# Selected attention: GpSimd weighs two of the four selected heads, and ScalarE's selected exponentials are split around the first window copies

## The chip, the core and the metric

One core of a Trainium2 chip runs the whole program: TensorE (PE, with its weight loads as PEld), VectorE (DVE), ScalarE (ACT), GpSimd (POOL) and SyncE (SP), each with its own instruction queue, tied together by semaphores. The metric is the device time of one execution in microseconds (us); smaller is better.

## The reference

The input (512 tokens of width 1024, float32) goes through two blocks of differential attention with a conformer convolution, and then through a block that mixes a gated delta rule with native sparse attention (NSA), projects, and ends in a squared-ReLU MLP. The change touches only the NSA part: 16 query heads in 4 groups of 4, head width 64.

```python
o_cmp = einsum(softmax(s_c) * any_valid, vc)          # compressed keys
o_slc = selection_branch(q, k_s, v_s, sel_idx, slopes) # selected blocks of 64 keys
o_win = window_branch(q, k_w, v_w, slopes)             # the last 256 keys
gates = sigmoid(gate_logits).reshape(B, S, G, R, 3)
o = gates[..., 0:1] * o_cmp + gates[..., 1:2] * o_slc + gates[..., 2:3] * o_win
```

With 512 keys there are 8 blocks and 8 are selected, so the selected branch is full causal attention. Each branch's softmax is divided by its sum and multiplied by its gate; the kernel does both with one factor per query and head ("weighing") before the probabilities go to PE.

## The kernel before

The NSA attention runs over 16 units, `units[u] = (g, t)`: a head group g of 0 to 3 and, inside it, a tile t of 128 queries, 0 to 3. A unit has 128(t+1) selected keys, at most 384 window keys and 31 compressed ones, for 4 heads (`REP`). Each engine's program is written out by hand, and the engines work one unit apart: while PE, and ACT's copies, finish unit u, DVE and ACT prepare unit u+1.

- DVE, for unit u+1: `gate_copy(u-1)` (the gate products of PE out of PSUM, L2886); `selected_in` (scores out of PSUM with the slope added, L2826, then the negated row maximum, L2810 and L2815); `window_in` (the same for the window and the compressed keys, L2841 to L2853, whose two `tops_ready` counts release ACT); `weigh` of the selected branch, then of the window and of the compressed keys (1/sum, L2865; times the gate, L2868; then four TENSOR_SCALARs over the heads, L2879, or one TENSOR_TENSOR, L2875). I call a period what lies between two gate copies.
- ACT: copies of unit u's transposed selected probabilities from PSUM (L2178), the four selected exponentials of unit u+1 in place with their row sums (L2121), the copies of unit u's window and compressed transposes, the four window exponentials of u+1, the copy of u's output (L2187), the compressed exponentials (L2117), and after every second unit the cast of a gate weight panel (L1710).
- PE: `selected_scores(u+1)` (L1447), then `selected_out(u)`: transposes of p_slc (L1466), a piece of a gate product (L743 to L745, `gate_fill`), `window_scores(u+1)` (L1456, L1457) ahead of the last selected block, and the products with the values (L1479). Then `window_out(u)` does the same for window and compressed keys, with pieces of the gate product between, and the rest of the gate product follows. A gate product's first piece waits for `gate_copied`.
- POOL: only `lower`: for each weight panel two TENSOR_TENSORs (L2965) that make its low part `wlo` from the panel and ACT's rounded `whi`. Panels `PN_GATE` to `PN_GATE+7` (indices 26 to 33) hold the gate weights; `lower(N0+pn+2)` makes panel pn+2.

ACT casts panel 27 after the last product ahead of this stage, just before unit 0; POOL's `lower` of it follows that cast. In the last unit ACT also casts the first four chunks of the delta rule's output (`dn_upper`, L2193), for POOL's `odn_lo` (L3147).

## Time and profile before

| | |
|---|---|
| median of 3 timed runs | 2678.96 us (2669.74, 2679.64, 2678.96) |
| profiled execution, time | 2668.49 us |
| its span, first to last instruction | 2666.7 us |
| busy share of the span | PE 95%, DVE 43%, ACT 37%, POOL 50% |
| NSA stage (1906 to 2153 us of the span) | 247.0 us: PE busy 232.1, DVE 198.7, ACT 151.1, POOL 42.8 |

Times of instructions are microseconds from the span's start. A busy share counts the union of an engine's instructions; on PE their ends are modelled, so a busy PE need not be at its peak. "Idle before" an instruction is put down to the engine and line whose semaphore came last. The timed runs lie at two levels about 10 us apart, and the profiled execution lies at the lower one.

### The profile page before, as it was taken

How to read it: one execution, taken by the hardware profiler on the slowest of the kernel's cores; microseconds unless marked ns; L12 is line 12 of the kernel's file. 1: busy time of each engine (PE TensorE's matmuls, PEld its weight loads, DVE VectorE, ACT ScalarE, POOL GpSimd, SP SyncE). 2: the span in 40 equal slices, each digit the busy share in tenths (PEclk: the TensorE clock that was granted, in tenths of full speed). 3: DMA queues.
4: the chain of work that ended last, by engine and by line, in shares of the span. 5: the costliest groups of instructions: out<-in, count | busy, mean ns of one | idle time of the engine just before them, and what ended most of it. 6: DMA issues, size and time to landing. Idle time of an engine off the chain costs nothing.

```text
span 2666.7 us, 42605 instructions
## 1 busy us (share of the span) xinstructions
PE 2533.1 (95%) x16743; PEld 2155.2 (81%) x16743; DVE 1141.7 (43%) x2061; ACT 974.1 (37%) x1723; POOL 1323.6 (50%) x754
## 2 busy tenths in 40 slices
PE   7988999999998899999989899999999999999999
PEld 7967999999995788878768678888766677788887
DVE  6874422123687432112567645301588812320210
ACT  4344422223434442222355512332556652321221
POOL 4761766567676276656844411122211166564552
PEclk9997999999998899999989889899999999899999
DMA  5210222322321022232222200132111152222222
GB/s 163 70 58 17 64 94 75 99 95 70 105 80 48 17 80 94 83 106 83 91 64 81 94 2 2 33 111 64 52 53 63 48 182 79 79 95 95 95 96 77
DMA packets 175660, 203.70 MB, mean 76 GB/s; under 512 B 6435, under 2 KB 160646, under 8 KB 175254
## 3 DMA queue, kind: packets, MB, share of 16 engines
q1 hardware_dynamic: 172176, 199.57, 23.1%
q10 hardware_dynamic: 3334, 2.06, 0.3%
q8 instruction: 103, 1.69, 0.3%
q14 instruction: 47, 0.39, 0.0%
HBM read 193.23 MB, written 8.39 MB: 76 GB/s over the span
## 4 chain that ended last, share of the span: by engine, by line
PE 76%; DVE 8%; POOL 4%; ACT 3%; issue 3%; POOLq 2%; ACTq 1%; DVEq 1%; DMA 0%; SPq 0%
PE ps L743 18%; PE ps L744 17%; PE ps L745 17%; PE ps L1626 7%; PE ps L992 4%; POOL wlo L2965 3%; POOLq L3010 2%; ACTq L2123 1%; DVE s_top L2810 1%; PE ps L1431 1%; PE ps L1245 1%; POOL conv L3008 1%; PE ps L1215 1%; PE ps L1249 1%; DVE p_slc L2826 1%
## 5 line engine op out<-in xcount | busy, mean ns | idle before, releaser
L2965 POOL TENSOR_TENSOR wlo<-wraw,whi 128x1024 fp32r<-128x1024 f32 x364 | 878.9, 2436 | 836.5 <-ACT whi L1710 836.4
L743 PE MATMUL ps<-hn_hi,whi 128*128 128x264 f32 (+1 forms) x2400 | 829.9, 346 | 23.9 <-POOL wlo L2965 9.6
L744 PE MATMUL ps<-hn_lo,whi 128*128 128x264 f32 (+1 forms) x2400 | 816.9, 340 | 0.0
L745 PE MATMUL ps<-hn_hi,wlo 128*128 128x264 f32 (+1 forms) x2400 | 814.2, 339 | 0.0
L1710 ACT CAST whi<-wraw 128x2048 fp32r<-128x2048 f32 x182 | 346.5, 1904 | 534.4 <-PE ps L745 361.2
L743 PEld LDWEIGHTS ps<-hn_hi,whi 128*128 128x128 f32 x2400 | 454.7, 189 | 89.3 <-issue 24.1
L745 PEld LDWEIGHTS ps<-hn_hi,wlo 128*128 128x128 f32 x2400 | 454.7, 189 | 51.2
L744 PEld LDWEIGHTS ps<-hn_lo,whi 128*128 128x128 f32 x2400 | 455.3, 190 | 45.6
L743 PE MATMUL ps<-ff_hi,whi 128*128 128x264 f32 (+1 forms) x528 | 170.2, 322 | 5.8 <-POOL wlo L2965 5.8
L744 PE MATMUL ps<-ff_lo,whi 128*128 128x264 f32 (+1 forms) x528 | 169.6, 321 | 0.0
L745 PE MATMUL ps<-ff_hi,wlo 128*128 128x264 f32 (+1 forms) x528 | 169.4, 321 | 0.0
L2357 DVE SCALAR_TENSOR_TENSOR ps<-z,lay_conv,ps 128x528 f32<-128x528 f32 x174 | 134.3, 772 | 13.5 <-issue 0.4
L2539 DVE TENSOR_TENSOR glu_gate<-ps,rstd_rows 128x264 f32<-128x264 f32 (+1 forms) x66 | 33.9, 518 | 205.9 <-PE ps L745 196.9
L743 PEld LDWEIGHTS ps<-ff_hi,whi 128*128 128x128 f32 x528 | 99.3, 188 | 16.0 <-POOL wlo L2965 8.0
L3053 POOL TENSOR_TENSOR glu_gate<-glu_gate,rstd_rows 128x264 f32<-128x264 f32 (+1 forms) x66 | 61.1, 935 | 90.2 <-ACT glu_gate L1895 90.2
L745 PEld LDWEIGHTS ps<-ff_hi,wlo 128*128 128x128 f32 x528 | 99.4, 188 | 7.6
L744 PEld LDWEIGHTS ps<-ff_lo,whi 128*128 128x128 f32 x528 | 99.3, 188 | 7.5
L2546 DVE TENSOR_TENSOR glu_val<-ps,glu_gate 128x264 f32<-128x264 f32 (+1 forms) x66 | 34.3, 520 | 160.6 <-PE ps L745 158.8
L1626 PE MATMUL ps<-f_hi,whi 128*128 128x512 f32 (+1 forms) x256 | 101.5, 397 | 0.0
L1626 PE MATMUL ps<-f_hi,wlo 128*128 128x512 f32 (+1 forms) x256 | 101.1, 395 | 0.0
L1626 PE MATMUL ps<-f_lo,whi 128*128 128x512 f32 (+1 forms) x256 | 101.1, 395 | 0.0
L3057 POOL TENSOR_TENSOR ff_lo<-glu_val,ff_hi 128x264 f32 (+1 forms) x66 | 62.0, 946 | 69.6 <-DVE ff_hi L2549 69.6
(478 smaller groups left out, 4199.9 us busy)
## 6 DMA issues: line engine op xcount, KB each, us to landing
wraw<-in_w_in SPq DMA_DIRECT2D x54, 1024.0 KB, 5.2
wraw<-in_w_gate_up SPq DMA_DIRECT2D x44, 1024.0 KB, 5.1
wraw<-in_w_up SPq DMA_DIRECT2D x16, 1024.0 KB, 5.5
wraw<-in_w_down SPq DMA_DIRECT2D x16, 1024.0 KB, 4.8
wraw<-in_w_out SPq DMA_DIRECT2D x12, 1024.0 KB, 5.0
wraw<-in_w_down SPq DMA_DIRECT2D x16, 768.0 KB, 4.3
wraw<-in_w_down SPq DMA_DIRECT2D x16, 640.0 KB, 4.1
gate_dram<-gate_out SPq DMA_DIRECT2D x16, 256.0 KB, 2.2
```

The costliest lines, as they stand in the source:

```text
L743: nc.tensor.matmul(dst, whi[:, slot, c:c + P], rhs_hi, start=start, stop=False)
L744: nc.tensor.matmul(dst, whi[:, slot, c:c + P], rhs_lo, start=False, stop=False)
L745: return nc.tensor.matmul(dst, wlo[:, slot, c:c + P], rhs_hi, start=False, stop=stop)
L992: last = nc.tensor.matmul(dst, wt[:, j % 2, c:c + P], x, start=(k == 0 and i == 0), stop=(k == 3 and i == 2))
L1626: last = nc.tensor.matmul(ps[:, c, :], w[:, slot, w0:w0 + P], x, start=(first and j == 0), stop=False, skip_group_check=True)
L1710: nc.scalar.copy(whi[:, slot, :], wraw[:, slot, :]).then_inc(w_hi, 1)
L2357: last = nc.vector.scalar_tensor_tensor(conv_acc if j < TAPS - 1 else conv[:, c * T1:(c + 1) * T1], z[:, c, j:j + T1], lay_conv[:, 4 * j + ...
L2546: nc.vector.tensor_tensor(v, ps[:, 4 + j, 0:w], glu_piece(glu_gate, l, j, oc, w), ALU.mult).then_inc(glu_used, count)
L2965: last = nc.gpsimd.tensor_tensor(wlo[:, slot, part], wraw[:, slot, part], whi[:, slot, part].bitcast(F32), ALU.subtract)
L3010: pool.drain()
L3053: nc.gpsimd.tensor_tensor(g, g, rstd_rows[:, a:a + w], ALU.mult).then_inc(gate_rows, count)
L3057: nc.gpsimd.tensor_tensor(ff_lo[:, ds(i * 2 + oc, 1), a:a + w].rearrange(flat), glu_piece(glu_val, l, j, oc, w), ff_hi[:, ds(i * 2 + oc, 1 ...
```

## The change

Of the selected branch's weighing DVE keeps the factor and heads 0 and 1; POOL weighs heads 2 and 3. The factor (`weigh(u, B_SLC)`) moves into `window_in`, behind the window's negated top and ahead of the compressed keys' top. DVE's steps are counted by `weigh_step` (four a unit: factor, two heads, window, compressed), POOL's by `slc_weighed`; PE's `selected_out` waits for both. On ACT heads 0 and 1 of the selected exponentials come before the first two window copies (`window_copies(u, range(0, 2))`; for t = 0 and 1 the compressed copy counts as one of the positions), heads 2 and 3 behind them. In the last unit `dn_upper(range(0, 4))` moves behind the first two window copies. POOL's panels from 28 on are lowered behind the weighing of units 3, 5, ..., 15.

```diff
@@ PE
             def selected_out(u):
                 n = units[u][1] + 1
-                pe.wait_ge(p_weighed, 3 * u + 1)
+                pe.wait_ge(weigh_step, 4 * u + 2)
+                pe.wait_ge(slc_weighed, u + 1)
                 for b in range(min(n, 2)):
                     block_turned(u, "slc", p_slc[u % 2], b)
...
-                        pe.wait_ge(p_weighed, 3 * u + 3)
+                        pe.wait_ge(weigh_step, 4 * u + 4)
...
-                pe.wait_ge(p_weighed, 3 * u + 2)
+                pe.wait_ge(weigh_step, 4 * u + 3)
@@ ACT
-            def exponentials(u, part):
+            def exponentials(u, part, heads=range(REP)):
                 slot, (_, t) = u % 2, units[u]
-                act.wait_ge(tops_ready, 3 * u + part + 1)
+                if heads[0] == 0:
+                    act.wait_ge(tops_ready, 3 * u + part + 1)
...
-                    for r in range(REP):
+                    for r in heads:
                         nc.scalar.activation(p[:, r, 0:w], p[:, r, 0:w], ACT.Exp, bias=s_neg[:, slot, i, r:r + 1],
                                              scale=head_col(q_rstd, u, r), accum_out=s_mass[:, slot, i, r:r + 1])
-                act.drain().then_inc(exps_done, 1)
+                if heads[-1] == REP - 1:
+                    act.drain().then_inc(exps_done, 1)
...
+            def window_copies(u, blocks):
+                n = min(units[u][1] + 1, 3)
+                for b in blocks:
+                    if b < n:
+                        turned_copy(("win", u, b), p_t[:, turn_no["win", u, b] % 2, :], lambda bank: ps[:, bank, :])
+                    elif b == n:
+                        turned_copy(("cmp", u, 0), pc_t, lambda bank: ps[:, bank, 0:P])
...
                 block_copies(u, "slc", t + 1)
                 if u + 1 < UNITS:
-                    exponentials(u + 1, 0)
-                if u == UNITS - 1:
+                    exponentials(u + 1, 0, range(0, 2))
+                window_copies(u, range(0, 2))
+                if u + 1 < UNITS:
+                    exponentials(u + 1, 0, range(2, REP))
+                else:
                     dn_upper(range(0, 4))
-                block_copies(u, "win", min(t + 1, 3))
-                turned_copy(("cmp", u, 0), pc_t, lambda bank: ps[:, bank, 0:P])
+                window_copies(u, range(2, 4))
@@ DVE
                 scaled_top(u, B_WIN).then_inc(tops_ready, 1)
+                weigh(u, B_SLC)
                 nc.vector.tensor_reduce(s_neg[:, slot, B_CMP, :], cmp[:, :, 0:N_CMP], AX.X, ALU.max, negate=True)
...
                 dve.wait_ge(exps_done, 3 * u + step)
+                if branch == B_SLC and u:
+                    dve.wait_ge(slc_weighed, u)
...
-                nc.vector.tensor_tensor(factor, factor, own[:, branch, :], ALU.mult)
+                last = nc.vector.tensor_tensor(factor, factor, own[:, branch, :], ALU.mult)
+                if branch == B_SLC:
+                    last.then_inc(weigh_step, 1)
+                    return
                 dve.drain()
...
-                p, w = (p_slc[slot], P * (t + 1)) if branch == B_SLC else (p_win[slot], P * min(t + 1, 3))
-                for r in range(REP):
+                weighed_heads(p_win[slot], P * min(t + 1, 3), branch, REP)
+
+            def weighed_heads(p, w, branch, heads):
+                for r in range(heads):
                     last = nc.vector.tensor_scalar(p[:, r, 0:w], p[:, r, 0:w], s_weight[:, branch, r:r + 1], None, ALU.mult)
-                last.then_inc(p_weighed, 1)
+                last.then_inc(weigh_step, 1)
...
                     window_in(u + 1)
-                    weigh(u + 1, B_SLC)
+                    weighed_heads(p_slc[(u + 1) % 2], P * (units[u + 1][1] + 1), B_SLC, 2)
@@ GpSimd
-            for pn in range(PN_Z, PN_GATE + 7):
+            def weigh_selected(u):
+
+                p, w = p_slc[u % 2], P * (units[u][1] + 1)
+                pool.wait_ge(weigh_step, 4 * u + 1)
+                for r in range(2, REP):
+                    last = nc.gpsimd.tensor_scalar(p[:, r, 0:w], p[:, r, 0:w], s_weight[:, B_SLC, r:r + 1], None, ALU.mult)
+                last.then_inc(slc_weighed, 1)
+
+            for pn in range(PN_Z, PN_GATE):
                 lower(N0 + pn + 2, pn % 2)
+            for u in range(UNITS):
+                weigh_selected(u)
+                if u >= 3 and u % 2:
+                    pn = PN_GATE + (u - 3) // 2
+                    lower(N0 + pn + 2, pn % 2)
```

On POOL, from the delta rule's last step to the NSA stage, before: a row is an instruction (line, operation, out and in tiles by their names, shape, and the semaphores that it waits for). Panels 14 to 34 follow each other, two instructions each; the "..." stands for such pairs.

```order
L3126 TENSOR_TENSOR k_tok<-k_tok,ke_col 128x1024 [waits dw_done]
L2965 TENSOR_TENSOR wlo<-wraw,whi 128x1024 [waits w_hi]
L2965 TENSOR_TENSOR wlo<-wraw,whi 128x1024
...
L2965 TENSOR_TENSOR wlo<-wraw,whi 128x1024 [waits w_hi]
L2965 TENSOR_TENSOR wlo<-wraw,whi 128x1024
L3147 TENSOR_TENSOR odn_lo<-qkv,odn_hi 128x512 [waits o_hi_ready] x8
L2965 TENSOR_TENSOR wlo<-wraw,whi 128x1024 [waits w_hi]
L2965 TENSOR_TENSOR wlo<-wraw,whi 128x1024
L3147 TENSOR_TENSOR nq_lo<-nq,nq_hi 128x512 [waits o_hi_ready] x8
```

In the changed program the run of panels ends with panel 27, and POOL's next rows are these (lines are 22 or more higher; p_slc_194 and p_slc_195 are the two slots of selected probabilities). The row ISA stands once before, too, ahead of the program's first TENSOR_TENSOR, and is what the trace calls MODIFY_POOL_CONFIG there.

```order
L2987 TENSOR_TENSOR wlo<-wraw,whi 128x1024 [waits w_hi]
L2987 TENSOR_TENSOR wlo<-wraw,whi 128x1024
L3168 ISA
L3168 TENSOR_SCALAR p_slc_194<-p_slc_194,s_weight 128x128 [waits weigh_step]
L3168 TENSOR_SCALAR p_slc_194<-p_slc_194,s_weight 128x128
L3168 TENSOR_SCALAR p_slc_195<-p_slc_195,s_weight 128x256 [waits weigh_step]
L3168 TENSOR_SCALAR p_slc_195<-p_slc_195,s_weight 128x256
...
L3168 TENSOR_SCALAR p_slc_195<-p_slc_195,s_weight 128x512 [waits weigh_step]
L3168 TENSOR_SCALAR p_slc_195<-p_slc_195,s_weight 128x512
L2987 TENSOR_TENSOR wlo<-wraw,whi 128x1024 [waits w_hi]
L2987 TENSOR_TENSOR wlo<-wraw,whi 128x1024
```

What moved: the weighing of unit 0 stands behind the lowering of panel 27, with an ISA row between, and panel 28 stands behind unit 3.

On ACT, from the selected copies of unit 2 to the window exponentials of unit 3 (t = 3, 512 selected keys), before:

```order
L2178 COPY p_t<-ps 128x512 [waits pv2_done,p_turned] x3
L2121 ACTIVATE p_slc_195,s_mass<-p_slc_195,s_neg,n_rstd 128x512 [waits tops_ready]
L2121 ACTIVATE p_slc_195,s_mass<-p_slc_195,s_neg,n_rstd 128x512 x3
L2178 COPY p_t<-ps 128x512 [waits pv2_done,p_turned] x3
L2178 COPY pc_t<-ps 128x128 [waits pv2_done,p_turned]
L2121 ACTIVATE p_win_197,s_mass<-p_win_197,s_neg,n_rstd 128x384 [waits tops_ready]
L2121 ACTIVATE p_win_197,s_mass<-p_win_197,s_neg,n_rstd 128x384 x3
```

On ACT, the same place in the changed program:

```order
L2182 COPY p_t<-ps 128x512 [waits pv2_done,p_turned] x3
L2124 ACTIVATE p_slc_195,s_mass<-p_slc_195,s_neg,n_rstd 128x512 [waits tops_ready]
L2124 ACTIVATE p_slc_195,s_mass<-p_slc_195,s_neg,n_rstd 128x512
L2182 COPY p_t<-ps 128x512 [waits pv2_done,p_turned] x2
L2124 ACTIVATE p_slc_195,s_mass<-p_slc_195,s_neg,n_rstd 128x512 x2
L2182 COPY p_t<-ps 128x512 [waits pv2_done,p_turned]
L2182 COPY pc_t<-ps 128x128 [waits pv2_done,p_turned]
L2124 ACTIVATE p_win_197,s_mass<-p_win_197,s_neg,n_rstd 128x384 [waits tops_ready]
L2124 ACTIVATE p_win_197,s_mass<-p_win_197,s_neg,n_rstd 128x384 x3
```

What moved: two of the window copies stand between the two halves of the selected exponentials, and one window copy and the compressed copy behind them.

On DVE, from the maximum of unit 1's window scores to the window's weighing, before:

```order
L2810 TENSOR_REDUCE s_top<-p_win_197 128x4
L2848 TENSOR_TENSOR p_cmp_199<-p_cmp_199,n_rstd 128x4x31
L2815 TENSOR_TENSOR s_neg<-s_top,n_rstd 128x4
L2851 TENSOR_REDUCE s_neg<-p_cmp_199 128x4
L2853 TENSOR_TENSOR p_cmp_199<-p_cmp_199,s_neg 128x4x31
L2865 RECIPROCAL s_weight<-s_mass 128x4 [waits exps_done]
L2868 TENSOR_TENSOR s_weight<-s_weight,gates 128x4
L2879 TENSOR_SCALAR p_slc_195<-p_slc_195,s_weight 128x256 x4
L2865 RECIPROCAL s_weight<-s_mass 128x4 [waits exps_done]
L2868 TENSOR_TENSOR s_weight<-s_weight,gates 128x4
L2879 TENSOR_SCALAR p_win_197<-p_win_197,s_weight 128x256 x4
```

On DVE, the same place in the changed program:

```order
L2824 TENSOR_REDUCE s_top<-p_win_197 128x4
L2862 TENSOR_TENSOR p_cmp_199<-p_cmp_199,n_rstd 128x4x31
L2829 TENSOR_TENSOR s_neg<-s_top,n_rstd 128x4
L2882 RECIPROCAL s_weight<-s_mass 128x4 [waits slc_weighed,exps_done]
L2885 TENSOR_TENSOR s_weight<-s_weight,gates 128x4
L2866 TENSOR_REDUCE s_neg<-p_cmp_199 128x4
L2868 TENSOR_TENSOR p_cmp_199<-p_cmp_199,s_neg 128x4x31
L2901 TENSOR_SCALAR p_slc_195<-p_slc_195,s_weight 128x256 x2
L2882 RECIPROCAL s_weight<-s_mass 128x4 [waits exps_done]
L2885 TENSOR_TENSOR s_weight<-s_weight,gates 128x4
L2901 TENSOR_SCALAR p_win_197<-p_win_197,s_weight 128x256 x4
```

What moved: the selected factor (the first RECIPROCAL and the product with the gates) stands ahead of the compressed top and now waits for `slc_weighed` too; two TENSOR_SCALARs of four are left.

## Rows read from the trace of the kernel before

**Rows 1.** Four periods of one group: length, busy us (instructions) by engine, clock.

```profile
core 0: us, PE busy (x) PEld busy (x) DVE busy (x) ACT busy (x) POOL busy (x), PEclk, DMA share, GB/s
2030.78:2043.68 12.90, 12.12 (x77) 8.47 (x75) 11.52 (x37) 8.64 (x22) 0.00 (x0) 1.00 0.33 102
2043.68:2059.42 15.74, 14.78 (x89) 9.37 (x85) 14.21 (x38) 8.83 (x24) 4.70 (x2) 1.00 0.05 18
2059.42:2077.55 18.13, 16.83 (x110) 11.15 (x109) 15.53 (x37) 12.16 (x27) 0.11 (x1) 1.00 0.25 74
2077.55:2093.16 15.61, 15.25 (x99) 9.72 (x99) 11.07 (x38) 8.66 (x26) 4.63 (x2) 1.00 0.05 18
```

**Rows 2.** Waits of the stage, 1906:2153: total us, times, longest us.

```profile
POOL wlo L2965 <- ACT whi L1710: 206.6, 8, 40.5
...
DVE s_weight L2865 <- ACTq L2123: 18.9, 15, 3.0
...
PE ps L1479 <- ACT p_t L2178: 12.2, 12, 1.3
```

**Rows 3.** Timeline, DVE's waits for window exponentials in three periods: start us, us.

```profile
2041.09 0.18 DVE L2865 RECIPROCAL s_weight<-s_mass 128x4 f32<-128x4 f32 x1 [0.45 <-ACTq L2123]
...
2056.55 0.18 DVE L2865 RECIPROCAL s_weight<-s_mass 128x4 f32<-128x4 f32 x1 [0.60 <-ACTq L2123]
...
2090.53 0.18 DVE L2865 RECIPROCAL s_weight<-s_mass 128x4 f32<-128x4 f32 x1 [2.90 <-ACTq L2123]
```

**Rows 4.** Timeline of the period before unit 11 (t = 3), PE, ACT and DVE.

```profile
2065.38 0.82 ACT L2121 ACTIVATE p_slc<-p_slc,s_neg,n_rstd 128x512 f32<-128x512 f32 x1 [2.07 <-DVE s_neg L2815]
...
2066.46 1.04 PE L1466 MATMUL ps<-const,p_win 128*128 128x128 f32 x8
...
2068.84 1.07 ACT L2178 COPY p_t<-ps 128x512 f32<-128x512 f32 x2 [0.15 <-issue]
...
2069.48 0.65 PE L1479 MATMUL ps<-p_t,vw 128*64 128x256 f32 x4 [1.30 <-ACT p_t L2178]
...
2070.22 0.16 DVE L2815 TENSOR_TENSOR s_neg<-s_top,n_rstd 128x4 f32<-128x4 f32 x1
...
2071.76 0.71 ACT L2121 ACTIVATE p_win<-p_win,s_neg,n_rstd 128x384 f32<-128x384 f32 x1
...
2074.68 0.18 DVE L2865 RECIPROCAL s_weight<-s_mass 128x4 f32<-128x4 f32 x1 [1.67 <-ACTq L2123]
```

**Rows 5.** DVE's selected weighing: duration ns min/median/max, forms.

```profile
L2879 DVE TENSOR_SCALAR p_slc<-p_slc,s_weight x64: 279/383/489, 1900.2 to 2134.9; 128x128 f32<-128x128 f32 x16, 128x256 f32<-128x256 f32 x16, 128x384 f32<-128x384 f32 x16, 128x512 f32<-128x512 f32 x16
```

**Rows 6.** Timeline at the stage's start, PE and POOL.

```profile
1906.60 0.66 PE L1466 MATMUL ps<-const,p_slc 128*128 128x128 f32 x4
...
1907.35 4.73 POOL L2965 TENSOR_TENSOR wlo<-wraw,whi 128x1024 fp32r<-128x1024 f32 x2 [7.24 <-ACT whi L1710]
```

**Rows 7.** Line L2965 at the program's start: duration ns, first and last start.

```profile
L2965 POOLq MODIFY_POOL_CONFIG  x2: 11/11/11, 0.8 to 0.9; - x2
```

**Rows 8.** Timeline of POOL at the program's start.

```profile
18.94 2.36 POOL L2965 TENSOR_TENSOR wlo<-wraw,whi 128x1024 fp32r<-128x1024 f32 x1 [18.06 <-ACT whi L1710]
```

**Rows 9.** POOL's groups by form: count, busy us, mean ns of one.

```profile
L3053 POOL TENSOR_TENSOR glu_gate<-glu_gate,rstd_rows 128x264 f32<-128x264 f32 x44 | 32.7, 754 | 43.8 <-ACT glu_gate L1895 43.8
...
L3083 POOL TENSOR_TENSOR hn_lo<-t,hn_hi 128x512 fp32r<-128x512 f32 x16 | 20.5, 1292 | 6.1 <-ACT hn_hi L1930 6.0
...
L3121 POOL COPY keys_queries<-qkv 128x512 f32<-128x512 f32 x8 | 4.7, 613 | 32.3 <-PE ps L1249 32.3
```

**Rows 10.** Windows of a pause of PE and of what follows, columns as in rows 1.

```profile
873.64:877.80 4.16, 0.00 (x0) 0.00 (x0) 2.01 (x5) 4.04 (x10) 2.40 (x2) 0.50 0.00 0
877.80:883.20 5.40, 5.37 (x53) 2.49 (x54) 1.34 (x4) 1.59 (x5) 2.70 (x2) 0.50 0.00 0
```

**Rows 11.** Timeline, a DVE operation with two SBUF inputs beside POOL's lowering.

```profile
2077.44 4.75 POOL L2965 TENSOR_TENSOR wlo<-wraw,whi 128x1024 fp32r<-128x1024 f32 x2 [28.90 <-ACT whi L1710]
...
2080.11 2.09 DVE L2815 TENSOR_TENSOR s_neg<-s_top,n_rstd 128x4 f32<-128x4 f32 x1
```

**Rows 12.** Timeline of the last unit, ACT and PE.

```profile
2144.74 2.18 ACT L2193 CAST odn_hi<-qkv 128x512 fp32r<-128x512 f32 x4
...
2149.96 0.65 PE L1479 MATMUL ps<-p_t,vw 128*64 128x256 f32 x4
```

More of the change, by code:

```diff
@@ L479, in hybrid_blocks @@
         win_read = sem("win_read")
-        p_weighed = sem("p_weighed")
+        weigh_step = sem("weigh_step")
+        slc_weighed = sem("slc_weighed")
         o_taken = sem("o_taken")
@@ L2874, in weigh @@
                     p = p_cmp[slot][:, :, 0:N_CMP]
-                    nc.vector.tensor_tensor(p, p, wide(factor, [P, REP, N_CMP], 2), ALU.mult).then_inc(p_weighed, 1)
+                    nc.vector.tensor_tensor(p, p, wide(factor, [P, REP, N_CMP], 2), ALU.mult).then_inc(weigh_step, 1)
                     return
-                p, w = (p_slc[slot], P * (t + 1)) if branch == B_SLC else (p_win[slot], P * min(t + 1, 3))
-                for r in range(REP):
+                weighed_heads(p_win[slot], P * min(t + 1, 3), branch, REP)
+            def weighed_heads(p, w, branch, heads):
+                for r in range(heads):
                     last = nc.vector.tensor_scalar(p[:, r, 0:w], p[:, r, 0:w], s_weight[:, branch, r:r + 1], None, ALU.mult)
-                last.then_inc(p_weighed, 1)
+                last.then_inc(weigh_step, 1)
             def gate_copy(f):
@@ L2889, in _ @@
             window_in(0)
-            weigh(0, B_SLC)
+            weighed_heads(p_slc[0], P * (units[0][1] + 1), B_SLC, 2)
             for u in range(UNITS):
```

## The prediction

> **What bounds the kernel now.** The page gives PE 95% of the span, so I look for where PE or what feeds it waits inside the stage that the change touches. The table of periods [rows 1] shows two things: PE is busy 12.12 of 12.90, 14.78 of 15.74, 16.83 of 18.13 and 15.25 of 15.61 us, so little can be won in a period; and DVE, at 11.52, 14.21 and 15.53 in the first three, is nearly as full. The waits [rows 2] say what is left: DVE waits 18.9 us in all for ACT's window exponentials (ACTq L2123), and PE 12.2 us for ACT's copies of the transposes, each at most 1.3. POOL idles 206.6 us. The loop that sets a period is then: gate copy, selected_in and window_in on DVE, window exponentials on ACT, window weighing on DVE, next gate copy. DVE waits for the exponentials 0.45 us before units with t = 1, 0.60 with t = 2, 2.90 with t = 0 [rows 3] and 1.67 with t = 3 [rows 4], and just ahead of this wait, in program order, stands the selected weighing.
>
> In three of the four periods the window exponentials start as soon as the negated window top is there or as PE has delivered the transposes. In the period into t = 3 they do not: the top (s_neg) is done at 2070.38, the exponentials begin at 2071.76, because ACT first runs the four selected exponentials (2065.38 to 2068.84) and then the window copies of the unit before, while PE, whose transposes began at 2066.46, stands 1.30 us at 2069.48 for the first copy [rows 4].
>
> **The change, part by part.**
>
> *Two heads off DVE.* 32 TENSOR_SCALARs of 0.28 to 0.49 us, median 0.38 [rows 5]: 32 x 0.38 = 12.2 us of DVE. They stand ahead of the wait for the window exponentials in every period, so DVE waits longer by what it saves. I cost the removal at 0; the cover is the wait [rows 3, 4].
>
> *The exponentials split.* In the period into t = 3, with 0.83 us for one of four exponentials ((2068.84 - 0.15 - 2065.38)/4): heads 0 and 1 end at 2067.0; the first copy needs the first block's transposes, about 2066.46 + 0.7 = 2067.15, and the pair takes 1.07, to 2068.2; heads 2 and 3 with the drain end at 2069.95. PE, freed by the first copy, no longer waits its 1.30 at 2069.48, so the third block is turned by then; third and compressed copy take about 0.75, and the window exponentials start at 2070.7 instead of 2071.76. That is 1.06 us sooner, of a possible 1.38 [rows 4]. Four such periods: -4.2 us. Into t = 1 and 2 PE's copies come sooner too, but the loop through DVE's top is as long as before: 0. Into t = 0 the copies wait for PE and the second pair goes behind them; DVE's weighing then waits up to 1.5 us, which the 2.90 us covers: 0 (up to 0.5 a period if that cover were gone).
>
> *DVE's new wait.* The wait for the selected exponentials moves ahead of the compressed top; the window exponentials are released before it, the compressed ones run last on ACT, so 0. In this time POOL's two TENSOR_SCALARs run. The trace shows none on POOL. The nearest rows at 512 columns are a copy, one input, 0.613 us, and a TENSOR_TENSOR, two inputs, 1.292 [rows 9]. A TENSOR_SCALAR has one tensor as input; I take 0.7. DVE operations can be held by POOL's: the s_neg that takes 0.16 alone [rows 4] took 2.09 us and ended at 2082.20, as POOL's lowering (to 2082.19) did [rows 11]. The compressed top's last operation has two SBUF inputs of this kind, and DVE's two heads stand behind it. Into t = 3 POOL begins near 2070.9 and ends at 2072.3 with 0.7 each; DVE's heads then end near 2073.2, and the exponentials near 2073.6: no loss. With 1.292 each POOL ends at 2073.5 and DVE at 2074.4, which takes back 0.8 of the 1.06. I put +0.4 on the sum for the whole stage, ends 0 and +5 (0.8 x 4 and 0.4 x 4 into t = 2).
>
> The Trainium skill (SBUF — State Buffer, Who interferes with whom) says that VectorE shares a port pair with GpSimd as an exclusive lock, taken by operations with two SBUF inputs and by TENSOR_SCALARs in their two-port mode; the 2.09 us [rows 11] agrees for the first kind; by the second kind DVE's two heads, too, would queue behind POOL's, which no run here shows yet.
>
> *POOL's queue at the stage's start.* This is the costly part. Before, PE's first transposes of p_slc started at 1906.60, and POOL's lowering of panel 27 ran from 1907.35 to 1912.08 [rows 6], with nobody waiting. Now unit 0's heads 2 and 3 stand behind that lowering in POOL's queue, and PE waits for them before its first transpose; behind PE's wait stand the gate product and unit 1's window scores, and for those DVE and then ACT. Nothing covers it: 1912.08 - 1906.60 = 5.48 us.
>
> *The ISA row.* Between the lowering and the first TENSOR_SCALAR POOL gets a second MODIFY_POOL_CONFIG. Before, it stands once, at 0.8 us [rows 7], and POOL's next operation that is not a memset starts at 18.94, after 18.06 us of idle that ended with ACT's cast [rows 8]. So the trace bounds its cost by 0 and 18.06 us. The upper end contains the wait for the first weights, so I go below the middle (9.0) and take 7 us. All of it lies on PE's wait.
>
> The Trainium skill (GPSIMD Engine Reference, 2.1 Instruction dispatch) gives about 6 us for the first call of a freshly loaded GpSimd kernel; no run here shows it, and by it the sum would be 1 us lower.
>
> *Unit 0's two weighings*, 128 columns: by the form of 264 columns (0.754, two inputs) and the copy's rate (0.613 x 128/512 = 0.15) between 0.15 and 0.5 each; I take 0.3, together 0.6.
>
> *The clock.* PE pauses 5.48 + 7 + 0.6 = 13.1 us. After a pause of 4.16 us PE worked 5.40 us at a granted clock of 0.50, 1.2 GHz [rows 10]. The same 5.40 us here would cost up to 2.7 us; I take 2.0, ends 0 and 2.7.
>
> *The last unit.* The four odn_hi casts (2.18 us) move from 2144.74 to behind the first two window copies, so the third copy comes that much later, which PE's products at 2149.96 need [rows 12]: about +0.6. POOL's odn_lo has slack.
>
> Later panels are due a unit later and POOL idles 206.6 us [rows 2]: 0.
>
> **The sum**: 5.5 + 7.0 + 0.6 + 2.0 - 4.2 + 0.4 + 0.6 = +11.9 us. Against the profiled execution's 2668.49 us that is 2680.4. The median of the runs, 2678.96, is 10.5 us above that execution; at that level the sum is 2690.9. Which level the next median takes I can't tell; I give 2686, between the two.
>
> **The rivals.** (a) *The stall is dearer*: the reload costs 8.5 us or more, or POOL's TENSOR_SCALARs cost more than a TENSOR_TENSOR, so that every period grows. For it: the 18.06 us bound, and that no row shows the operation; against it: the copy's 0.613. With 12 us of reload: +16.9, 2685 at the lower level, 2696 at the upper. It decides from a reload of 8.5 us on (+13.4). (b) *The reload is free*, as the same configuration was loaded at 0.8 us: +4.9, 2673 to 2684. (c) *No stall*: POOL's queue gets through the panel and the reload before PE needs it, if the cast of panel 27 came sooner. Only the gains stay: -4.2 + 1.0 = -3.2, 2665 to 2676. Against it: that cast follows the last product ahead of the stage [rows 6]. (d) *Clearly faster*: no stall, and all of PE's idle time in the stage goes, 247.0 - 232.1 = 14.9 us: 2654 to 2664. Against it: PE's waits for the copies are 12.2 us in all [rows 2], and DVE's loop stays as long in three of four periods.
>
> **The numbers.** A measurement here tells about 0.5%, 13.4 us, from no change. My forecast 0.44, (a) 0.42, (b) 0.07, (c) 0.04, (d) 0.03. The forecast, (b) and (c) are within 0.5%: 0.55; (a) slower: 0.42; (d) faster: 0.03. The range goes from (b) at the lower level, cut a little, 2675, to (a) at the upper, 2699.
>
> **What would show it.** Right: one PE gap of about 13 us ended by POOL at the first p_slc transpose, MODIFY_POOL_CONFIG between panel 27 and the first TENSOR_SCALAR, a stretch at clock 0.50 after it; the periods into t = 3 near 17.1 us, the others at 12.9, 15.7 and 15.6; DVE's waits for ACTq longer, not gone; the stage near 259 us instead of 247.0. Wrong: no long PE gap there (then (b) or (c)); POOL's TENSOR_SCALARs above 1.3 us at 512 columns, or DVE operations of 1 us and more beside them in every period (then (a)); periods into t = 1 and 2 that shorten by what DVE saved, 0.6 to 0.8 us, which would say that DVE's removal was on the path.

## The result: 0.7% slower, and the profile after

The kernel after takes 2696.02 us at the median of 13 runs (2683.37 to 2703.55), the kernel before, beside it, 2677.84: the ratio is 1.0073 with a 95% interval of 1.0058 to 1.0089, some 19.5 us more. That is above the 0.5% that tell a difference from no change, and inside the range of 2675 to 2699. One of the 13 runs of the kernel before, at 3120.55 us, lies far above the others and is not in the ratio.

The profiled execution has a span of 2697.8 us against 2666.7. Of these 31.1 us, 13.4 lie ahead of the stage (unit 0's selected scores start at 1918.92 instead of 1905.53), where both kernels do the same work. Of the 13.4, 9.7 arise behind 1690 us: three stretches at a granted clock of 0.50 are 10.2 us long there, where before two of 3.4 us stood and no third. One kernel below was profiled twice and has the three long stretches in one execution (e7) and the two short ones in the other (e2), so they are no part of the change. The stage itself, from those scores to the last gate copy, grew by 17.7 us, which is near what the timed runs give. It splits in two: 8.5 us up to the first gate copy (21.81 us instead of 13.29), and 9.2 us in the fifteen periods behind it (245.16 instead of 235.95).

**The start.** The profile after, timelines of PE and of POOL, the instructions of POOL's weighing line (duration ns min/median/max, first and last start), and a window with the columns of [rows 1]:

```profile
1926.78 1.09 PE L1467 MATMUL ps<-const,p_slc 128*128 128x128 f32 x4 [6.72 <-POOL p_slc L3168]
```

```profile
1920.75 4.64 POOL L2987 TENSOR_TENSOR wlo<-wraw,whi 128x1024 fp32r<-128x1024 f32 x2 [7.24 <-ACT whi L1712]
1925.45 1.19 POOL L3168 TENSOR_SCALAR p_slc<-p_slc,s_weight 128x128 f32<-128x128 f32 x2
```

```profile
L3168 POOL TENSOR_SCALAR p_slc<-p_slc,s_weight x32: 603/1146/1902, 1925.4 to 2163.2; 128x128 f32<-128x128 f32 x8, 128x256 f32<-128x256 f32 x8, 128x384 f32<-128x384 f32 x8, 128x512 f32<-128x512 f32 x8
L3168 POOLq MODIFY_POOL_CONFIG  x2: 17/18/18, 1925.3 to 1925.4; - x2
```

```profile
1924.00:1931.30 7.30, 4.52 (x19) 3.58 (x21) 0.70 (x3) 1.76 (x5) 2.58 (x3) 0.53 0.00 0
```

PE, which began its transposes without a wait in [rows 6], now stands 6.72 us for POOL. The wait began at 1926.78 - 6.72 = 1920.06; the lowering of panel 27 ended at 1925.39, 5.33 us later; the pair of weighings takes 1.19. Between the two stand both MODIFY_POOL_CONFIGs and 0.06 us. Then PE works on at a clock of 0.53, and at the first gate copy the delay has grown from 6.7 to 8.5 us. Not all of this growth is the clock's: in e3 below, which has the same wait of 6.72 us and a like stretch at 0.50 but no split, the delay at the first gate copy is 7.55 us.

**The periods.** Four periods of the kernel after, the ones of [rows 1]:

```profile
2056.53:2069.42 12.89, 12.89 (x83) 9.01 (x79) 11.50 (x35) 8.63 (x23) 1.86 (x2) 1.00 0.33 102
2069.42:2085.16 15.74, 15.16 (x88) 9.33 (x86) 13.99 (x36) 9.10 (x25) 7.43 (x4) 1.00 0.05 18
2085.16:2104.32 19.16, 16.04 (x101) 10.46 (x101) 17.80 (x35) 12.53 (x28) 6.02 (x4) 1.00 0.23 70
2104.32:2121.43 17.11, 16.38 (x95) 10.22 (x97) 8.93 (x36) 7.51 (x24) 3.49 (x3) 0.90 0.05 17
```

The periods into t = 1 and t = 2 are what they were. The one into t = 3 grew from 18.13 to 19.16 us, and in it DVE is busy for 17.80 us where it was for 15.53, though two of its operations left. The one into t = 0 grew from 15.61 to 17.11 at a clock of 0.90. All four periods into t = 3 are 19.1 to 19.2 us. Of the four periods right behind them (three into t = 0, and the last) the first did not grow; the others did, by 1.9, 1.5 and 2.1 us, and 0.65 of the last are the moved odn_hi casts (below).

Into t = 3, timeline of DVE, ACT, POOL and PE of the kernel after, and its groups on POOL by form (count, busy us, mean ns of one):

```profile
2096.93 3.57 POOL L3168 TENSOR_SCALAR p_slc<-p_slc,s_weight 128x512 f32<-128x512 f32 x2 [14.43 <-DVE s_weight L2885]
2097.10 0.65 DVE L2868 TENSOR_TENSOR p_cmp<-p_cmp,s_neg 128x124 f32<-128x124 f32 x1
...
2097.68 1.22 DVE L2901 TENSOR_SCALAR p_slc<-p_slc,s_weight 128x512 f32<-128x512 f32 x2
...
2099.11 0.18 DVE L2882 RECIPROCAL s_weight<-s_mass 128x4 f32<-128x4 f32 x1 [0.22 <-ACTq L2127]
...
2099.61 1.75 DVE L2901 TENSOR_SCALAR p_win<-p_win,s_weight 128x384 f32<-128x384 f32 x4
2099.89 1.91 ACT L1712 CAST whi<-wraw 128x2048 fp32r<-128x2048 f32 x1 [0.15 <-issue]
...
2101.87 4.75 POOL L2987 TENSOR_TENSOR wlo<-wraw,whi 128x1024 fp32r<-128x1024 f32 x2 [1.38 <-ACT whi L1712]
...
2102.11 2.28 DVE L2895 TENSOR_TENSOR p_cmp<-p_cmp,s_weight 128x124 f32<-128x124 f32 x1
...
2104.32 0.68 DVE L2908 COPY gate_out<-ps 128x512 f32<-128x512 f32 x1
...
2105.05 0.53 PE L744 MATMUL ps<-hn_hi,whi 128*128 128x512 f32 x1 [2.44 <-DVE gate_out L2908]
```

```profile
L3168 POOL TENSOR_SCALAR p_slc<-p_slc,s_weight 128x512 f32<-128x512 f32 x8 | 13.8, 1730 | 56.6 <-DVE s_weight L2885 56.6
...
L3168 POOL TENSOR_SCALAR p_slc<-p_slc,s_weight 128x128 f32<-128x128 f32 x8 | 4.7, 606 | 26.7 <-DVE s_weight L2885 26.6
```

The window exponentials do start sooner: DVE's reciprocal behind them stands 13.95 us after the gate copy (2099.11 - 2085.16) instead of 15.26, and the split's gain of 1.31 is there. It is lost behind it. POOL's pair at 512 columns takes 3.57 us and reaches to 2100.50, under DVE's window weighing, which takes 1.75 us. The cast on ACT follows the exponentials, not DVE, so POOL's lowering starts at 2101.87, and DVE's compressed weighing, at 2102.11, is 0.24 us behind it. It takes 2.28 us. The same two operations of DVE in the kernel before, timeline:

```profile
2075.18 1.41 DVE L2879 TENSOR_SCALAR p_win<-p_win,s_weight 128x384 f32<-128x384 f32 x4
...
2077.34 0.29 DVE L2875 TENSOR_TENSOR p_cmp<-p_cmp,s_weight 128x124 f32<-128x124 f32 x1
```

There the compressed weighing stood 0.10 us ahead of the lowering of [rows 11] and took 0.29 us. This is a race between DVE and POOL. Counted from the start of the window weighing, the lowering starts 2.26 us later in both kernels; the compressed weighing starts 2.16 us later before and 2.50 us later now, and the difference is the 0.34 us by which the window weighing is held. In the other three periods into t = 3 the window weighing takes 1.41 us (behind 0.41 us of idle time), 1.57 and 1.57, and the compressed weighing starts 0.24, 0.06 and 0.06 us behind the lowering. The gate copy waits for the compressed weighing, and PE 2.44 us for the gate copy; right behind, from 2105.4, PE works 3.4 us at a clock of 0.50.

### The profile page after: what moved, and what is told of

The parts are those of the page before. It is cut to its first block, busy times and chain, and to the rows that moved or that the text cites. A ratio compares the mean times of both kernels' runs of the same rounds, so it can differ in the third digit from the quotient of the medians.

```text
span 2697.8 us, 42607 instructions
## 1 busy us (share of the span) xinstructions
PE 2553.4 (95%) x16743; PEld 2168.0 (80%) x16743; DVE 1146.0 (42%) x2029; ACT 972.4 (36%) x1723; POOL 1359.5 (50%) x786
## 4 chain that ended last, share of the span: by engine, by line
PE 76%; DVE 8%; POOL 4%; ACT 4%; issue 3%; POOLq 2%; DVEq 2%; ACTq 1%; DMA 1%; SPq 0%
PE ps L744 18%; PE ps L745 17%; PE ps L746 17%; PE ps L1628 7%; PE ps L993 4%; POOL wlo L2987 3%; POOLq L3032 2%; ACTq L2127 1%; DVE s_top L2824 1%; PE ps L1432 1%; PE ps L1246 1%; ACT whi L1712 1%; PE ps L1250 1%; PE ps L1216 1%; PE ps L1214 1%
## 5 line engine op out<-in xcount | busy, mean ns | idle before, releaser
L3168 POOL TENSOR_SCALAR p_slc<-p_slc,s_weight 128x128 f32<-128x128 f32 (+3 forms) x32 | 36.8, 1162 | 160.2 <-DVE s_weight L2885 160.2
L744 PEld LDWEIGHTS ps<-ff_hi,whi 128*128 128x128 f32 x528 | 99.3, 188 | 16.7 <-POOL wlo L2987 8.7
```

What stands on the lines that cost most here:

```text
L744: nc.tensor.matmul(dst, whi[:, slot, c:c + P], rhs_hi, start=start, stop=False)
L3168: last = nc.gpsimd.tensor_scalar(p[:, r, 0:w], p[:, r, 0:w], s_weight[:, B_SLC, r:r + 1], None, ALU.mult)
```

## The experiments

The start is the time from unit 0's selected scores to the first gate copy, the periods that from the first to the last gate copy, both from each kernel's profile; the sum is against before's 249.24 us.

```
kernel                    start   periods  sum     ratio to before, 95% interval
before                    13.29   235.95           
after                     21.81   245.16   +17.7   1.0073 [1.0058, 1.0089]
e1_unit0_first            13.29   246.70   +10.7   1.0044 [1.0019, 1.0069]
e3_pool_only              20.84   238.36   +10.0   1.0043 [1.0023, 1.0063]
e4_lower_late             21.68   232.49    +4.9   1.0035 [1.0014, 1.0055]
e5_order_and_late         13.29   232.54    -3.4   1.0002 [0.9983, 1.0021]
e2_split_only             13.29   231.31    -4.6   1.0001 [0.9981, 1.0021]
e7_split_again (same)     13.30   231.29    -4.7   0.9983 [0.9967, 0.9999]
e6_dve_late_before        13.29   262.86   +26.9   one run, 2707.76 us
e8_pool_tensor_tensor     13.29   232.67    -3.3   one run, 2675.61 us
e9_pool_tt_lower_free     13.29   253.03   +17.1   1.0046 [1.0031, 1.0061]
```

**Unit 0's weighing ahead of panel 27** (e1):

```diff
-            for pn in range(PN_Z, PN_GATE):
+            for pn in range(PN_Z, PN_GATE - 1):
                 lower(N0 + pn + 2, pn % 2)
-            for u in range(UNITS):
+            weigh_selected(0)
+            lower(N0 + PN_GATE + 1, (PN_GATE - 1) % 2)
+            for u in range(1, UNITS):
```

> The changed kernel with one thing moved: POOL's weighing of unit 0's heads 2 and 3 stands ahead of the lowering of panel 27 in its queue. Theory (queue order): the 6.7 us PE gap at the stage's start was the panel ahead of the weighing, and the half clock after it 1.8 us more; both go, the first gate copy comes some 8 us sooner than in the changed kernel, no PE gap over 2 us stands there, and the total is about +10 us against the kernel before (+17.7 in the stage less 8). Rival (reload): the reload of POOL's program has a price that was hidden behind the wait for the cast; then a gap of several us before the first TENSOR_SCALAR stays, and the total stays near +17.

The start is back at 13.29 us, with no wait of PE for POOL. The profile of e1, timeline of POOL and instructions of the weighing line:

```profile
1904.93 4.75 POOL L2987 TENSOR_TENSOR wlo<-wraw,whi 128x1024 fp32r<-128x1024 f32 x2 [9.37 <-ACT whi L1712]
1909.81 1.19 POOL L3168 TENSOR_SCALAR p_slc<-p_slc,s_weight 128x128 f32<-128x128 f32 x2
1916.92 4.72 POOL L2987 TENSOR_TENSOR wlo<-wraw,whi 128x1024 fp32r<-128x1024 f32 x2 [5.93 <-ACT whi L1712]
```

```profile
L3168 POOLq MODIFY_POOL_CONFIG  x2: 6/6/6, 1909.6 to 1909.7; - x2
```

Here nothing but the row of the configuration stands between the lowering of panel 26 (to 1909.68) and the first TENSOR_SCALAR: 0.13 us. In e8 below, where POOL uses TENSOR_TENSORs and the trace has no MODIFY_POOL_CONFIG at this place, 0.11 us stand between the same two. The whole 8.5 us were the order of the queue and what followed from it, the clock included; the reload has no price that these rows show. The periods keep the loss: 10.7 us, more than the 9.2 of the kernel after, because here the period behind the first one into t = 3 grew too.

**POOL's weighing without the split** (e3): exponentials, then all copies, as before.

```diff
-                    exponentials(u + 1, 0, range(0, 2))
-                window_copies(u, range(0, 2))
-                if u + 1 < UNITS:
-                    exponentials(u + 1, 0, range(2, REP))
-                else:
+                    exponentials(u + 1, 0)
+                if u == UNITS - 1:
                     dn_upper(range(0, 4))
-                window_copies(u, range(2, 4))
+                block_copies(u, "win", min(t + 1, 3))
+                turned_copy(("cmp", u, 0), pc_t, lambda bank: ps[:, bank, 0:P])
```

> The changed kernel without ScalarE's split: only the weighing of two heads on POOL. Theory (the cast that comes earlier puts POOL's lowering ahead of DVE's compressed weighing): without the split the cast and the lowering are late again, the compressed weighing takes 0.3 us instead of 2.3, the periods into t = 3 are near 18.1 and those into t = 0 near 15.6, and only the start's 8.5 us stays: about +8.5 against the kernel before. Rival (POOL's slow weighing is itself on the path of every period into t = 3): these periods stay at 19 us or more, and the total is +13 or above.

Three of the four periods into t = 3 are 18.1 us, the first is 20.46: +10.0 for the stage, of which 7.55 are the start. The rival falls, but the first period was not foreseen. The profile of e3, timeline of DVE and POOL in the first and in the third of these periods:

```profile
1956.52 1.41 DVE L2899 TENSOR_SCALAR p_win<-p_win,s_weight 128x384 f32<-128x384 f32 x4 [0.41 <-issue]
...
1958.45 4.74 POOL L2985 TENSOR_TENSOR wlo<-wraw,whi 128x1024 fp32r<-128x1024 f32 x2 [3.22 <-ACT whi L1712]
...
1958.68 2.28 DVE L2893 TENSOR_TENSOR p_cmp<-p_cmp,s_weight 128x124 f32<-128x124 f32 x1
...
2085.89 0.29 DVE L2893 TENSOR_TENSOR p_cmp<-p_cmp,s_weight 128x124 f32<-128x124 f32 x1
2085.99 4.74 POOL L2985 TENSOR_TENSOR wlo<-wraw,whi 128x1024 fp32r<-128x1024 f32 x2 [2.87 <-ACT whi L1712]
```

0.10 us ahead of the lowering the weighing takes 0.29 us, 0.23 behind it 2.28. What made it late the first time is 0.41 us of idle time on DVE for which the trace has no releaser; it stands at this one place in all the kernels with weighing on POOL, and its cause stays open. The kernels with all four heads on DVE have 0.43 us of such idle time in the same period, but ahead of the product of the selected factor and the gate, where DVE comes to wait for the window exponentials anyway. Without the split POOL's pair has ended before DVE's window weighing starts, so nothing is held there. With the split the window weighing comes 1.3 us sooner, under the pair. Neither part alone loses the race, except where those 0.41 us stand; together they lose it in every period into t = 3.

**The lowering held back** (e4, the kernel after; e5, with unit 0 first as well):

```diff
                 if u >= 3 and u % 2:
                     pn = PN_GATE + (u - 3) // 2
+                    pool.wait_ge(weigh_step, 4 * u + 4)
                     lower(N0 + pn + 2, pn % 2)
```

> The changed kernel with POOL's lowering of the stage's panels held back until DVE's compressed weighing of that unit is done. Theory (the lowering holds the compressed weighing 2.0 us): the compressed weighing takes 0.3 us, PE's 2.4 us gaps at the gate products and the half clock after them go, the periods into t = 3 are near 17.2 us and into t = 0 near 15.6, and the total is about +5 to +9 us against the kernel before (start +8.5, split up to -4). Rival: the weighing by POOL's TENSOR_SCALARs alone is what costs; then the periods into t = 3 stay at 18.5 or more and the total at +14 or above.

> The changed kernel with both mends at once: unit 0's weighing ahead of the lowering of panel 27, and the stage's lowerings held back until DVE's compressed weighing of that unit is done. Theory (these two account for all that the change lost): first transposes of p_slc to first gate copy 12.2 us as in the kernel before, first to last gate copy 232.5 us as with the late lowering alone, so -3.5 us against the kernel before, ratio near 0.9987. Rival (the weighing on POOL costs something of its own that neither mend touches): the total stays above the kernel before.

The profile of e4, timeline into t = 3 (PE, DVE, POOL):

```profile
2082.05 1.75 DVE L2901 TENSOR_SCALAR p_win<-p_win,s_weight 128x384 f32<-128x384 f32 x4
...
2084.55 0.29 DVE L2895 TENSOR_TENSOR p_cmp<-p_cmp,s_weight 128x124 f32<-128x124 f32 x1
2084.76 0.68 DVE L2908 COPY gate_out<-ps 128x512 f32<-128x512 f32 x1
2084.93 4.69 POOL L2987 TENSOR_TENSOR wlo<-wraw,whi 128x1024 fp32r<-128x1024 f32 x2 [1.99 <-DVE p_cmp L2895]
...
2085.50 0.50 PE L744 MATMUL ps<-hn_hi,whi 128*128 128x512 f32 x1 [0.43 <-DVE gate_out L2908]
```

One wait on POOL takes 12.7 us off the periods (245.16 to 232.49): those into t = 3 are 17.0 to 17.2, PE's wait is 0.43 instead of 2.44, and no stretch at half clock is left in the periods. The window weighing is still held (1.75), so the first hold costs little by itself and much by the second one that it brings about. With both mends the stage is 3.4 us shorter than before, as expected; the timed runs (1.0002, with an interval of 0.9983 to 1.0021) cannot tell that from nothing.

**The split alone** (e2, and e7, the same kernel again): ACT's lines of the change in the kernel before, DVE weighing all four heads.

> The kernel before with ScalarE's split alone; DVE weighs all four selected heads. Theory: the window exponentials start 1.3 us sooner in the four periods into t = 3, nothing stands against it, and the periods into t = 3 are near 17.0 us instead of 18.13; total about -4 to -5 us against the kernel before, ratio near 0.998. Rival (the split costs): the second pair behind the copies delays the selected weighing, and with it the chain, in the other periods, above all into t = 0; then the total is at or above the kernel before.

> ScalarE's split alone, once more, beside the kernel with both mends. Theory: -4.6 us in the stage, ratio near 0.998, some 1 us less than the kernel with both mends, since POOL's pair holds up DVE's window weighing by 0.15 to 0.35 us a unit there. Rival: at or above the kernel with both mends, which would say that taking two heads off DVE is worth something.

Both profiles show -4.6 to -4.7 us in the stage. The timed runs do not settle it: the first set gave 1.0001, the second 0.9983 with an interval that ends at 0.9999. Four periods of e7, and what DVE waited for ACT's exponentials between e7's first and last gate copy (total us, times, longest):

```profile
2031.80:2044.70 12.90, 12.90 (x81) 8.97 (x80) 11.53 (x37) 8.63 (x22) 0.00 (x0) 1.00 0.33 102
2044.70:2060.44 15.74, 15.55 (x91) 9.70 (x89) 14.20 (x38) 9.18 (x25) 4.70 (x2) 1.00 0.05 18
2060.44:2077.26 16.82, 15.42 (x97) 10.06 (x98) 15.54 (x38) 11.48 (x26) 0.11 (x1) 1.00 0.25 80
2077.26:2092.86 15.60, 15.50 (x101) 9.97 (x101) 11.15 (x38) 8.69 (x26) 4.63 (x2) 1.00 0.05 18
```

```profile
DVE s_weight L2877 <- ACTq L2125: 13.1, 16, 2.0
```

Only the period into t = 3 is shorter, by 1.31, four times 1.3 in all; the last period is 0.65 longer (15.23 instead of 14.58), where the odn_hi casts stand behind the first copies. And e5, which differs from e7 only by the two heads on POOL with both mends, is 1.25 us longer in the profiled stage (the intervals of the timed runs overlap). Taking the heads off DVE shows no gain even with its faults mended: DVE waits longer for ACT's exponentials, 16.7 us in e5 between the same two copies where e7 has 13.1.

**DVE 0.34 us later, in the kernel before** (e6): the sum over the compressed exponentials stands twice in units with t = 3.

```diff
                 if branch == B_CMP:
+                    if t == 3:
+                        nc.vector.reduce_sum(mass_of, p_cmp[slot][:, :, 0:N_CMP], AX.X)
+                        dve.drain()
                     nc.vector.reduce_sum(mass_of, p_cmp[slot][:, :, 0:N_CMP], AX.X)
```

> The kernel before, with DVE's sum over the compressed exponentials done twice in the units with t = 3, which makes its compressed weighing some 0.34 us later and leaves everything else. Theory (a race of 0.1 us for the port): the weighing, which started 0.10 us ahead of POOL's lowering, now starts 0.24 behind it and takes 2.3 us instead of 0.29; the periods into t = 3 go from 18.13 to about 20.4, PE waits over 2 us at the gate product, and the period into t = 0 behind it may grow by 1.5 for the clock. Rival (DVE only queues in the order of its own work): 0.34 us a period, 18.5.

The direction was right and the size was not: these periods went from 18.1 (the last from 18.4) to 22.7 us, by 4.4 to 4.6 and not 2.3. The profile of e6, timeline of DVE, POOL and PE:

```profile
2101.38 0.28 DVE L2866 TENSOR_REDUCE s_mass<-p_cmp 128x4 f32<-128x124 f32 x1
...
2101.95 4.65 POOL L2968 TENSOR_TENSOR wlo<-wraw,whi 128x1024 fp32r<-128x1024 f32 x2 [29.22 <-ACT whi L1710]
2101.98 2.34 DVE L2871 TENSOR_TENSOR s_weight<-s_weight,gates 128x4 f32<-128x4 f32 x1
2104.40 2.35 DVE L2878 TENSOR_TENSOR p_cmp<-p_cmp,s_weight 128x124 f32<-128x124 f32 x1
...
2107.40 0.80 PE L743 MATMUL ps<-hn_hi,whi 128*128 128x512 f32 x1 [4.96 <-DVE gate_out L2889]
```

The lowering is two instructions, and two of DVE's operations with both inputs in SBUF now fall behind them, one behind each half: the product of factor and gate, 128x4, which takes 0.17 us alone, and the weighing. None of the change is in this kernel: 0.34 us of DVE work cost up to 4.6 us a period and 26.9 in the stage, 8.2 of them in the periods right behind, where the clock is below 1.00.

**POOL by TENSOR_TENSORs** (e8, as e5; e9, as e1, where the lowering is free):

```diff
-                    last = nc.gpsimd.tensor_scalar(p[:, r, 0:w], p[:, r, 0:w], s_weight[:, B_SLC, r:r + 1], None, ALU.mult)
+                    last = nc.gpsimd.tensor_tensor(p[:, r, 0:w], p[:, r, 0:w], s_weight[:, B_SLC, r:r + 1].to_broadcast([P, w]), ALU.mult)
```

> The kernel with both mends, where POOL weighs its two heads by TENSOR_TENSORs with the factor spread along the columns in place of TENSOR_SCALARs. If the TENSOR_SCALAR's own price is what was mis-sized, the pair at 512 columns falls from 3.4 us to about 2.6 (1.29 each, as the rows of the kernel before have for 512 columns), and DVE's window weighing is not held; if what it shares with DVE's work beside it makes it slow, the pair stays near 3.4.

> The kernel with unit 0's weighing first and POOL weighing by TENSOR_TENSORs (2.08 us a pair at 512 columns instead of 3.4), but with the lowering free to start as soon as its cast is done. Theory (the 0.34 us by which POOL's long pair holds DVE's window weighing is what puts the compressed weighing behind the lowering): the shorter pair ends before the window weighing, which takes 1.41 us again, the compressed weighing starts 0.1 us ahead of the lowering, and three of the four periods into t = 3 are near 16.9; the first one, with the 0.41 us of idle time that every kernel with weighing on POOL showed ahead of the window weighing there, is 19 us or more; total near the kernel before. Rival (the earlier cast of the split puts the lowering ahead whatever POOL's pair takes): all four stay at 19.1, stage 246, ratio near 1.004.

The profile of e8, instructions of the weighing line, and of e9, timeline of DVE and POOL in the second period into t = 3:

```profile
L3168 POOL TENSOR_TENSOR p_slc<-p_slc,s_weight x32: 400/742/1085, 1912.1 to 2143.6; 128x128 f32<-128x128 f32 x8, 128x256 f32<-128x256 f32 x8, 128x384 f32<-128x384 f32 x8, 128x512 f32<-128x512 f32 x8
```

```profile
2025.11 1.65 DVE L2901 TENSOR_SCALAR p_slc<-p_slc,s_weight 128x512 f32<-128x512 f32 x2
...
2027.16 1.41 DVE L2901 TENSOR_SCALAR p_win<-p_win,s_weight 128x384 f32<-128x384 f32 x4
2027.32 1.91 ACT L1712 CAST whi<-wraw 128x2048 fp32r<-128x2048 f32 x1
...
2029.30 4.72 POOL L2987 TENSOR_TENSOR wlo<-wraw,whi 128x1024 fp32r<-128x1024 f32 x2 [3.22 <-ACT whi L1712]
2029.33 2.47 DVE L2895 TENSOR_TENSOR p_cmp<-p_cmp,s_weight 128x124 f32<-128x124 f32 x1
```

DVE's two selected heads in that period of e9 (duration ns min/median/max, first and last start):

```profile
L2901 DVE TENSOR_SCALAR p_slc<-p_slc,s_weight x2: 474/866/1259, 2025.1 to 2026.3; 128x512 f32<-128x512 f32 x2
```

With the TENSOR_TENSOR the price falls from 1.73 us at 512 columns to at most 1.09, yet e8's periods take 232.67 us, e5's 232.54: once the lowering is held back, POOL's own speed does not matter. In e9 the pair is short, the window weighing is free at 1.41 us, and the race is lost all the same: the periods into t = 3 are 21.41, 19.13, 21.41 and 19.11. In the two of 21.41 the product of factor and gate falls behind the lowering as well, as in e6. So neither the theory nor the rival came out whole, and the 0.34 us on the window weighing are not the only way into the loss. The two heads that stayed on DVE now take 1.65 us (the first 1.26 beside POOL's TENSOR_TENSOR, the second 0.47), as much as four did in e2 (1.67), DVE comes to the window weighing without a wait, and the compressed weighing starts 0.03 us behind the lowering. What stands is the wider statement: POOL's weighing delays DVE against ACT by some tenths, at one place or another, and the margin is 0.10. In e9 the total is +0.46%, some 12 us, less than the 17.1 us of its profiled stage; how many of these races the other runs lose is not shown, since only one execution of each kernel was profiled.

## Why the prediction was right and wrong

The time came out inside the range and 10 us above the forecast of 2686. No measurable change had 0.55 and slower 0.42; slower came. The sum was +11.9, the stage's growth is +17.7. That they are as near as this is luck: a term of 7 us that was not there, and 13.9 us in the periods where the sum had 0.4, are two errors of opposite sign. In measured terms the stage is 8.5 at the start, -4.7 for the split with the last unit, and 13.9 for the weighing on POOL in the periods.

- *POOL's queue at the start*, 5.48 us: right, 5.33 measured, and e1 took it away whole.
- *The ISA row*, 7 us: wrong. In the kernel after 0.06 us stand there, in e1 0.13. The bounds were 0 to 18.06 us, and the upper one came from a wait for the first weights; the value near its middle had no row behind it. By the 0.06 us the sum loses the whole term. Rival (b), the free reload, had the start right. The Trainium skill (GPSIMD Engine Reference, 2.1 Instruction dispatch) gives about 6 us for the first call of a freshly loaded kernel; these runs do not show it.
- *Unit 0's two weighings*, 0.6 us: 1.19.
- *The clock*, 2.0 us: 8.5 - 6.7 = 1.8 behind the wait at the start, near it; by e3, which has 0.83 there, 1.0 of the 1.8 comes in with the split. That the clock would fall again behind the periods into t = 3 was not in the sum.
- *The split*, -4.2 us: right in the mechanism, 1.31 instead of 1.06 a period, and *the last unit*, +0.6: 0.65. Together they make -4.6 us in the stage where the split stands alone (e2, e7).
- *Two heads off DVE*, 0: right, by e5 against e7. DVE's waits for ACT's exponentials did not go.
- *DVE's new wait*, +0.4 (ends 0 and +5): this step failed. "No loss" into t = 3 rested on 0.7 us for a TENSOR_SCALAR and ended where DVE's two heads end; measured is 1.73 us, dearer than the TENSOR_TENSOR of 1.292 that was the upper bound. But the price is not what cost (e8, e9). What the step did not follow is the race behind it: it read the hold of s_neg by the lowering [rows 11] and did not look at which operation stood just ahead of that lowering. The rows had it: the lowering started at 2077.44 [rows 11], and the gate copy, which follows the compressed weighing, at 2077.55 [rows 1]. Weighing with the split takes 245.16 - 231.30 = 13.9 us more in the periods than the split alone: 9.0 into t = 3, where the holds are, and 4.8 in the periods right behind, where PE works 3.4 us at half the clock after its wait. e4 takes back all but 1.2 of it.

Rival (a) named POOL's TENSOR_SCALARs dearer than a TENSOR_TENSOR, "so that every period grows". The condition came true, the mechanism did not: the periods into t = 1 and 2 have not grown, and those into t = 3 grew by the lowering. That its sum with a reload of 12 us, +16.9, is near the +17.7 is luck too: the traces show no reload that takes time. The signs that the prediction set out said so: no 13 us but 6.7 of PE's wait, TENSOR_SCALARs above 1.3 us, and one DVE operation of 2.3 us beside POOL.

The Trainium skill (SBUF — State Buffer, Who interferes with whom) says that of VectorE and GpSimd whoever issues first holds the shared pair for its whole instruction. The traces agree for VectorE's operations with two SBUF inputs beside POOL's lowering: 0.29 us at 0.10 ahead, 2.28 at 0.24 behind, and one operation behind each half in e6. A TENSOR_SCALAR of DVE, of which the prediction's second kind speaks, is held too: 1.26 us beside POOL's TENSOR_TENSOR in e9, where the next takes 0.47. Beside POOL's TENSOR_SCALARs the traces differ from the page: the hold is 0.65 instead of 0.29 and 1.75 instead of 1.41, some 0.35 us each, while the POOL instruction lasts 1.7.

## What to carry to other kernels

Before work is put on GpSimd, list the VectorE operations with two SBUF inputs that start within half a microsecond of a long GpSimd instruction, and on which side: here the place 0.1 us ahead of a 2.4 us instruction was worth 2 us, and anything that delays VectorE by a few tenths against the engine that releases GpSimd spends them. A wait of the long instruction for the short one made the order safe, at no price that e4 shows, since GpSimd had slack. And a piece of work that another engine will wait for belongs ahead of the bulk work in an in-order queue; measure each part alone first: the half of this change that needed no new engine gave all of the gain that the profiled stage shows.

## What the runs showed of the hardware that was not expected

- A TENSOR_SCALAR on POOL with a factor per partition (0.61 us at 128 columns, 1.73 at 512) is slower than the TENSOR_TENSOR with the factor spread over the columns (0.40 and up to 1.09), in the same place.
- Ahead of POOL's first TENSOR_SCALAR, with the MODIFY_POOL_CONFIG between, 0.06 us (after) and 0.13 us (e1) pass behind the lowering; without it, ahead of a TENSOR_TENSOR, 0.11 us (e8).
- 0.34 us more on VectorE in four of 16 units made a stage of 249 us 26.9 us longer (e6).
- In the periods of the kernel after PE's granted clock fell to 0.50 for 3.4 us behind three of its four waits of 2.4 to 3.2 us. It did not behind the first of them (2.43 us), nor behind one of 2.69 us in the same place of e3, but it did behind the one of 2.45 us there in e1; and it never fell in the periods of e2, e4, e5 and e7, where no wait of PE was above 1.2 us.
